# Feed-forwards of a six-layer network: the activations move past loaded weight blocks in five of six column groups

## What is computed

```python
def swiglu(h, w_in, w_out):
    gate, up = jnp.split(h @ w_in, 2, axis=-1)
    return (jax.nn.silu(gate) * up) @ w_out

x = x + 0.5 * rms_norm(swiglu(rms_norm(x, g[0]), ff1_w_in[i], ff1_w_out[i]), g[1])
...
x = x + rms_norm(m, g[3])
x = x + 0.5 * rms_norm(swiglu(rms_norm(x, g[4]), ff2_w_in[i], ff2_w_out[i]), g[5])
```

## Time and profile before

| | |
|---|---|
| median of 3 runs | 2987.64 us (2981.74 to 2991.76) |
| the profiled execution | 2977.27 us |
| its span, first to last instruction | 2975.5 us |
| PE busy | 2938.2 us (99%), 15397 matmuls |
| PE weight loads busy | 2487.7 us (84%) |
| DVE busy | 1804.8 us (61%) |
| ACT busy | 1464.1 us (49%) |
| DMA | 532.97 MB, mean 179 GB/s |

### The profile page before, as it was taken

One profiled execution on the slowest core, in us unless ns is written; L12 is line 12 of the kernel. 1 busy time (PEld: TensorE's weight loads), 2 busy tenths in 40 slices (PEclk: granted clock), 3 DMA queues, 4 the chain that ended last, 5 costly groups with the idle time before them and its releaser, 6 DMA issues.

```text
span 2975.5 us, 38371 instructions
## 1 busy us (share of the span) xinstructions
PE 2938.2 (99%) x15397; PEld 2487.7 (84%) x15397; DVE 1804.8 (61%) x2600; ACT 1464.1 (49%) x2133; POOL 69.3 (2%) x143
## 2 busy tenths in 40 slices
PE   8999999999999999999999999999999999999999
PEld 7889888888888888888888988897888889788887
DVE  6556655556655546765554665469775546977554
ACT  5445544435544444554543464354655434575542
POOL 0000000000000000000000000010000001000000
PEclk9999999999999999999999999999999999999999
DMA  7564555555555555265555635576244557625453
GB/s 247 185 215 134 177 184 193 190 190 199 186 189 181 194 186 191 97 204 185 191 186 182 225 128 186 184 206 214 100 156 156 185 182 208 214 86 184 154 185 129
DMA packets 302403, 532.97 MB, mean 179 GB/s; under 512 B 31074, under 2 KB 125204, under 8 KB 302228
## 3 DMA queue, kind: packets, MB, share of 16 engines
q1 hardware_dynamic: 288964, 511.63, 52.4%
q10 hardware_dynamic: 13264, 18.90, 1.8%
HBM read 528.33 MB, written 1.11 MB: 178 GB/s over the span
## 4 chain that ended last, share of the span: by engine, by line
PE 95%; DVE 2%; DMA 1%; ACT 1%; issue 1%; POOL 0%; ACTq 0%; SPq 0%; POOLq 0%; DVEq 0%
PE bank L744 90%; PE bank L1051 2%; PE bank L1091 1%; PE bank L829 1%; DMA sb_ring<-in_w_xq_dram 1%; DVE sb_parts L1867 0%; PE bank L804 0%; PE bank L812 0%; ACT sb_sc L1510 0%; DMA sb_ring<-in_w_in_dram 0%; ACT sb_parts L1365 0%; DMA sb_ring<-in_ff_w_in_dram 0%; DMA sb_arena<-in_norm_ffn_dram 0%; ACT sb_xn L1477 0%; DVE sb_oT_low L1990 0%
## 5 line engine op out<-in xcount | busy, mean ns | idle before, releaser
L1867 DVE TENSOR_TENSOR sb_parts<-sb_ring,sb_parts 128x2048 fp32r<-128x2048 f32 (+1 forms) x478 | 1092.2, 2289 | 781.6 <-ACT sb_parts L1365 779.6
L744 PE MATMUL bank<-sb_parts,sb_hT_high 128*128 128x512 f32 (+1 forms) x4480 | 1368.2, 391 | 0.7 <-ACT sb_hT_high L1339 0.6
L1365 ACT ACTIVATE sb_parts<-sb_ring 128x2048 fp32r<-128x2048 f32 (+1 forms) x478 | 911.0, 1913 | 812.9 <-PE bank L744 719.0
L744 PEld LDWEIGHTS bank<-sb_parts,sb_hT_high 128*128 128x128 f32 x4480 | 834.9, 188 | 178.8 <-issue 9.1
L744 PE MATMUL bank<-sb_parts,sb_hT_low 128*128 128x512 f32 (+1 forms) x2240 | 852.4, 390 | 0.0
L744 PE MATMUL bank<-sb_parts,sb_hidden_high 128*128 128x512 f32 x1760 | 543.5, 390 | 0.0
L744 PEld LDWEIGHTS bank<-sb_parts,sb_hT_low 128*128 128x128 f32 x2240 | 419.7, 188 | 87.5 <-DVE sb_hT_low L1990 0.5
L744 PEld LDWEIGHTS bank<-sb_parts,sb_hidden_high 128*128 128x128 f32 x1760 | 329.0, 188 | 68.0 <-issue 0.6
L744 PE MATMUL bank<-sb_parts,sb_hidden_low 128*128 128x512 f32 x880 | 342.6, 389 | 0.0
L744 PE MATMUL bank<-sb_hT_high,sb_parts 128*128 128x256 f32 x1408 | 254.9, 283 | 0.0
L744 PEld LDWEIGHTS bank<-sb_hT_high,sb_parts 128*128 128x128 f32 x1408 | 220.1, 192 | 0.0
(11 more groups left out here) (220 smaller groups left out, 1957.8 us busy)
## 6 DMA issues: line engine op xcount, KB each, us to landing
sb_ring<-in_ff_w_in_dram SPq DMA_DIRECT2D x160, 1024.0 KB, 5.1
sb_ring<-in_ff_w_out_dram SPq DMA_DIRECT2D x88, 1024.0 KB, 4.9
sb_ring<-in_w_gate_up_dram SPq DMA_DIRECT2D x40, 1024.0 KB, 5.1
sb_ring<-in_w_in_dram SPq DMA_DIRECT2D x38, 1024.0 KB, 5.1
sb_ring<-in_a_w_qkv_dram SPq DMA_DIRECT2D x24, 1024.0 KB, 5.2
sb_ring<-in_w_down_dram SPq DMA_DIRECT2D x22, 1024.0 KB, 4.9
sb_ring<-in_ff_w_in_dram SPq DMA_DIRECT2D x32, 512.0 KB, 4.9
sb_ring<-in_c_w_qkv_dram SPq DMA_DIRECT2D x12, 1024.0 KB, 5.0
```

Source lines behind the costliest of these rows:

```text
L744: return nc.tensor.matmul(o, lhsT, rhs, start=start, stop=stop)
L1365: nc.scalar.activation(halves(n, slice(0, filled(n))).high, ring[:, raw_in[n], 0:filled(n)], ACT.Copy) \
L1867: V.tensor_tensor(both.low, ring[:, raw_in[n], 0:filled(n)], both.high.bitcast(F32), ALU.subtract) \
```

## The change

In groups 1 to 5 blocks of weights are loaded and hT moves. hT.high and hT.low of a block of 128 now lie side by side in one tensor hT_both, so that one loaded block of high weights meets both in a single matmul of 512 columns: columns 0 to 255 of the bank get high x high, columns 256 to 511 get high x low. The third product, low weights with hT.high, is a matmul of 256 columns into the first half. The results lie in columns (128 hidden columns by 256 rows of x). A group's gate takes four banks j, one per block of 128 hidden columns, and so does its up. ACT copies the second half of a bank to SBUF (`low_half`), DVE adds the first (`gate_sum`, `up_sum`). The transposes of groups 1 to 5 are gone. Row factors in columns come from `turned_factors` (two transposes) and a copy to halves_f; they are multiplied in on the gate. The ups, group 0's included, go without them, and the factor is applied to the output y in `turn` instead. The gate takes its banks from a new list, (5, 6, 7, 4), all four before its first matmul; the up takes all of G.

```diff
-        hT = Split(sb("hT_high", [P, KD, S], F32R), sb("hT_low", [P, KD, S], F32R))
+        hT_both = sb("hT_both", [P, KD, 2, S], F32R)
+        hT = Split(hT_both[:, :, 0, :], hT_both[:, :, 1, :])
...
+        GATE, GATE_AFTER_MEMORY = (Banks(psum, which, owner, taken, readers) for which in ((5, 6, 7, 4), (4, 5, 7, 6)))
...
             def ffn(st):
                 first_rows(st, [(st, "first", h) for h in range(2)], lambda t: (st, "up", 0, t))
+                turned_factors(st, (st, "norm"), 2)
+                for t in range(NT):
+                    for b in range(KD // 2):
+                        pe.wait_ge(dve_read.sem, dve_read.at(((st, "norm"), t, b)))
                 for g in range(1, GROUPS_F):
                     for kind in ("gate", "up"):
-                        banks = [G.take(pe, (st, kind, g, t)) for t in range(NT)]
+                        banks = [((GATE_AFTER_MEMORY if st[0] == "ff3" else GATE) if kind == "gate" else G).take(pe, (st, kind, g, j)) for j in range(4)]
                         for h in range(2):
                             ckey = (st, kind, g, h)
                             arrived(ckey)
                             s = view(ckey)
-                            for t in range(NT):
+                            for j in range(4):
+                                cols = slice(j * P, (j + 1) * P)
                                 for k in range(4):
-                                    ins = split_mm(banks[t][:, :], hT[:, 4 * h + k, t * P:(t + 1) * P], s[:, k, :],
-                                                   h == 0 and k == 0, h == 1 and k == 3)
+                                    kt = 4 * h + k
+                                    if kt:
+                                        mm(banks[j][:, 0:S], s.low[:, k, cols], hT.high[:, kt, :], False, False)
+                                    ins = mm(banks[j][:, :], s.high[:, k, cols], hT_both[:, kt, :, :], kt == 0, kt == KD - 1)
+                                    if kt == 0:
+                                        ins = mm(banks[j][:, 0:S], s.low[:, k, cols], hT.high[:, kt, :], False, False)
...
-                            if kind == "gate" and h == 0:
-                                turned_hidden(st, g - 1, YB)
+                            if g == 1 and kind == "gate" and h == 0:
+                                turned_hidden(st, 0, G)
...
-            def squares(src, c, key):
+            def squares(src, c, key, factor=1.0):
...
+                def low_half(kind, g, j):
+                    act.wait_ge(matmul_done.sem, matmul_done.at((st, kind, g, j)))
+                    last_read = (kind, g, j - 2) if j > 1 else ("gate", g, j + 2) if kind == "up" else ("up", g - 1, j + 2)
+                    if last_read[1]:
+                        act.wait_ge(dve_read.sem, dve_read.at((st, *last_read)))
+                    copy(halves_f[:, j % 2, :], G.of((st, kind, g, j))[:, S:2 * S]).then_inc(act_read.sem, act_read.next((st, kind, g, j)))
...
-                    V.scalar_tensor_tensor(hid_f[:, t, 0:S], G.of((st, "up", 0, t))[:, S:2 * S], row_factor_of(st, t),
-                                           silu[:, t, 0:S], ALU.mult, ALU.mult) \
+                    V.tensor_tensor(hid_f[:, t, 0:S], G.of((st, "up", 0, t))[:, S:2 * S], silu[:, t, 0:S], ALU.mult) \
                         .then_inc(dve_read.sem, dve_read.next((st, "up", 0, t)))
+                factors_in(st, halves_f[:, 6, :])
+
+                def gate_sum(g, j):
+                    dve.wait_ge(act_read.sem, act_read.at((st, "gate", g, j)))
+                    if (g, j) > (1, 1):
+                        dve.wait_ge(act_step.sem, act_step.at((st, "silu", *((g, j - 2) if j > 1 else (g - 1, j + 2)))))
+                    one = halves_f[:, 2 + j % 2, :]
+                    settle(dve, V.tensor_tensor(one, G.of((st, "gate", g, j))[:, 0:S], halves_f[:, j % 2, :], ALU.add),
+                           dve_read, (st, "gate", g, j))
+                    V.tensor_tensor(one, one, halves_f[:, 6, :], ALU.mult).then_inc(dve_step.sem, dve_step.next((st, "summed gate", g, j)))
+
+                def up_sum(g, j):
+                    dve.wait_ge(act_read.sem, act_read.at((st, "up", g, j)))
+                    one = halves_f[:, 4 + j % 2, :]
+                    settle(dve, V.tensor_tensor(one, G.of((st, "up", g, j))[:, 0:S], halves_f[:, j % 2, :], ALU.add),
+                           dve_read, (st, "up", g, j))
+                    dve.wait_ge(act_step.sem, act_step.at((st, "silu", g, j)))
+                    V.tensor_tensor(one, one, silu_columns[:, j, :], ALU.mult).then_inc(dve_step.sem, dve_step.next((st, "hidden", g, j)))
+
+                def low_of(g, j):
+                    dve.wait_ge(act_step.sem, act_step.at((st, "hid high", g, j)))
...
+                def hidden_columns(g):
+                    up_sum(g, 0)
+                    up_sum(g, 1)
+                    low_of(g, 0)
+                    up_sum(g, 2)
+                    low_of(g, 1)
+                    up_sum(g, 3)
+                    low_of(g, 2)
+                    low_of(g, 3)
```

More of the change, by code:

```diff
@@ L1371, in squares_free @@
                     act.wait_ge(squared.sem, squared.count)
-            def squares(src, c, key):
+            def squares(src, c, key, factor=1.0):
                 squares_free()
-                nc.scalar.activation(junk, src, ACT.Square, accum_out=ssum[:, c:c + 1]).then_inc(squared.sem, squared.next(key))
+                nc.scalar.activation(junk, src, ACT.Square, scale=factor, accum_out=ssum[:, c:c + 1]).then_inc(squared.sem, squared.next(key))
             def norm_high(st, t):
@@ new lines, in silu_of @@
+                def silu_of(g, j):
+                    act.wait_ge(dve_step.sem, dve_step.at((st, "summed gate", g, j)))
+                    if g == 1:
+                        act.wait_ge(dve_read.sem, dve_read.at((st, "up", 0, 1)))
+                    else:
+                        act.wait_ge(dve_step.sem, dve_step.at((st, "hidden", g - 1, j)))
+                    nc.scalar.activation(silu_columns[:, j, :], halves_f[:, 2 + j % 2, :], ACT.Silu) \
+                        .then_inc(act_step.sem, act_step.next((st, "silu", g, j)))
@@ L1443, in ffn @@
                 for g in range(1, GROUPS_F):
                     ahead((st, "gate", g, 0))
-                    hidden_high(st, g - 1)
+                    if g == 1:
+                        hidden_high(st, 0)
+                    else:
+                        hidden_columns(g - 1)
                     ahead((st, "gate", g, 1))
-                    for t in range(NT):
-                        act.wait_ge(matmul_done.sem, matmul_done.at((st, "gate", g, t)))
-                        act.wait_ge(dve_read.sem, dve_read.at((st, "up", g - 1, t)))
-                        nc.scalar.activation(silu[:, t, :], G.of((st, "gate", g, t))[:, :], ACT.Silu, scale=row_factor_of(st, t)) \
-                            .then_inc(act_read.sem, act_read.next((st, "gate", g, t)))
@@ L1453, in ffn @@
-                    for h in range(2):
-                        ahead((st, "up", g, h))
+                    ahead((st, "up", g, 0))
+                    low_half("gate", g, 0)
+                    low_half("gate", g, 1)
+                    silu_of(g, 0)
+                    low_half("gate", g, 2)
+                    silu_of(g, 1)
+                    low_half("gate", g, 3)
+                    silu_of(g, 2)
+                    silu_of(g, 3)
+                    ahead((st, "up", g, 1))
                 for m in range(KF // 2 - 1):
@@ L1914, in times_gain @@
                             bank, key = output(st, t, h)
-                            V.tensor_tensor(xn[:, t, half], bank[:, :], gain_row[n % 2][:, half], ALU.mult) \
-                                .then_inc(dve_read.sem, dve_read.next(key))
+                            if st[0] == "mix":
+                                ins = V.tensor_tensor(xn[:, t, half], bank[:, :], gain_row[n % 2][:, half], ALU.mult)
+                            else:
+                                ins = V.scalar_tensor_tensor(xn[:, t, half], bank[:, :], row_factor_of(st, t), gain_row[n % 2][:, half],
+                                                             ALU.mult, ALU.mult)
+                            ins.then_inc(dve_read.sem, dve_read.next(key))
                         def first_half():
@@ L1938, in turn @@
                             dve.wait_ge(matmul_done.sem, matmul_done.at(key))
-                            settle(dve, V.tensor_tensor(x[:, t, half], x[:, t, half], bank[:, :], ALU.add), dve_read, key)
+                            if st[0] == "ff3":
+                                ins = V.scalar_tensor_tensor(x[:, t, half], bank[:, :], row_factor_of(st, t), x[:, t, half], ALU.mult, ALU.add)
+                            else:
+                                ins = V.tensor_tensor(x[:, t, half], x[:, t, half], bank[:, :], ALU.add)
+                            settle(dve, ins, dve_read, key)
```

(17 more changed lines are left out.)

40 lines of the change are left out of this document (28 added, 12 removed).

## The result

The change makes the kernel slower: 3016.43 us (median of 4 runs, 3003.2 to 3026.57) against 2984.69 us of the kernel before in the same rounds (4 runs, 2977.65 to 2991.76). The ratio is 1.0103, 95% interval [1.0074, 1.0133], +32 us. The forecast was 2986.1 us, no change, with a range of 2957 to 3012 us; the time lies above the range.

What follows compares the result with a forecast made beforehand. PE's own time was taken to bound the kernel. Matmuls +21, transposes -46, the bank wait +25 and a covered wait -1.5 made -1.5 us on 2987.64: 2986.1 us, eight-in-ten range 2957 to 3012 us.

Steps and rivals of the forecast that it cites:

- Ten times: +25 us.: Before group 1's gate PE waits for DVE's read of group 0's bank, once in each of ten feed-forwards: +25 us.
- 2.49 us: Length of PE's single wait for DVE's bank read before group 1's gate, 334.12 less 331.63.
- rival (a): The bank wait before group 1's gate costs nothing, because DVE's read comes earlier than today: 2961 us, chance 0.11.
- 320 x (0.2267 + 0.120) = 110.9 us: Matmuls of groups 1 to 5, per feed-forward: 320 pairs of 512 and 256 columns, against 108.8 us before: +2.1 us each.
- rival (d): Weight loads disturb the 256-column matmul slots of groups 1 to 5, ten ns each: 3018 us, chance 0.10.
- the 0.39 and 0.42 us that were allowed: Time per added 256-column operation, per group 16 on ACT (0.39 us) and 20 on DVE (0.42 us); cost nothing.
- (b): Alternating matmul lengths in groups 1 to 5 pack closer, 0.113 us a 256-column slot: 2964 us, chance 0.11.
- (c): DVE frees the up banks late, 1.2 us at 0.85 us an operation, 40 times, +48 us: 3034 us, chance 0.08.
- Rival (e): The 1,600 additional weight loads stay uncovered by matmuls: 3293 us, chance 0.02.
- the page's rule: Skill page: weight loads overlap matmuls in flight only in a different row group; 1,600 additional loads would cost 171 us.

Runs made afterwards that it cites:

- Experiment 2: Kernel before, plus one wait of PE for DVE's read of group 0's first up bank ahead of group 1's gate: 3018.04 us, ratio 1.0128.
- Experiment 1: Changed kernel with each bank taken right before its own first matmul, not all four ahead: 2969.44 us, ratio 0.9965 to the kernel before.
- experiment 7: Kernel before, with PE waiting ahead of group 1's gate only for ACT's earlier read of the same bank: 2989.14 us, ratio 1.0018.
- experiment 6: Changed kernel with banks taken one by one and, per chunk, sixteen long and sixteen short matmuls in runs: 2959.53 us, ratio 0.9928 to the kernel before.
- experiment 4: Changed kernel with banks taken one by one and matmuls of one length in runs of four: 2976.99 us, ratio 0.9973 to the kernel before.
- experiment 3: Changed kernel with matmuls of one length in runs of four, all four banks still taken ahead: 3007.1 us, ratio 1.0079 to the kernel before.

## Why the prediction was wrong, step by step

The forecast was -1.5 us and the medians say +32, so 33.5 us are missing. Two terms miss by about 16 us each, and the wait for L2074 adds 2. Either of the 16 alone would have left the time inside the range (2986 + 16 = 3002 us); both together carried it out.

**The step that failed: "Ten times: +25 us."** The working of this wait held in every part: its place, the bank, DVE last behind two splits, the reads at 0.42 us, and 23.3 us of idle time beside the "2.49 us" each. What failed is that the idle time was taken for the whole cost. Not counted was the clock, some 16 us at the medians, of which the traces put 7 directly behind the waits. None of the sum's terms, and no rival, had the granted clock in it. The trace of before has no idle stretch of PE of such a length within a feed-forward, and its clock is full in every slice; so its rows were silent on what a wait of 2.5 us does to the clock. The prediction bounded the pairs from both sides and the cost of this wait only from below (rival (a)). Experiment 2 shows that the wait does it: alone, in a kernel without pairs, it costs its 26 us and 10 us of clock directly behind it, and the kernel is as slow as the changed one. Experiment 1 takes it away and the stretches behind it are gone, and experiment 7 shows that waits of half the length bring none at these places. The Trainium skill (TensorE: Matmul & The Clock Gate, section HAM oscillation — how this bites in real kernels) tells of this mechanism, waits behind which TensorE starts at the lower clock. By its rule only longer gaps than those of this kernel would do so; the windows above disagree on that, since gaps of 2.3 to 2.7 us did it in some cases.

**The other step that failed, a term mis-sized: "320 x (0.2267 + 0.120) = 110.9 us".** This term, +21 us over ten feed-forwards, measured 351.7 ns a pair, that is +37 us, as much of the miss as the clock and the better shown of the two: experiment 6 gives 14 of the 16 us back. The prediction took the sum of two spacings that each came from a uniform run, and named the absence of a row for alternation. The excess of 5 ns lies inside its upper bound (ten ns, rival (d)), but the mechanism of that rival, loads in the way of 256 slots, is not supported: experiment 6 has exactly as many loads and short matmuls, in runs of sixteen, and goes at 347.3 ns, and in the changed kernel the 256 slots are not stretched at all (116.7 ns for 120). It is the change from short to long that costs, in the first five long matmuls behind it, which is why runs of four cost as much as alternation.

**Right.** The transposes fell to 4 a feed-forward. ACT's and DVE's added operations run at 369 to 425 ns, near the 0.39 and 0.42 us that were allowed, and PE doesn't wait for them at the later gates and ups, with one exception: before the up of group 3 of the first feed-forward it waits 2.2 us for L2074, the reads of group 2's up, since DVE did some 4 us of work of the kernel's start just ahead of them (78.3 to 82.3 us). Rivals (a), (b) and (c) are out: the wait was there, pairs were not closer, and DVE's last read was in time 39 times in 40. Rival (e), and the page's rule beside it, would have shown 171 us or more; pairs of 0.352 us leave no room for it.

**Put together at the medians.** Of +32 us, -9 are matmuls and transposes, +25 are waits, and the rest, about 16, is the clock. Part of that last term isn't settled. Four low stretches behind the waits cost 1.7 us each, 7 us. The remainder comes from low stretches in attention, far from any wait of L2058. By their mean clock about half of the executions of the kernel before have such stretches too, though no trace of one was taken. The changed kernel's profiled execution had two of 23.9 us, and those of experiments 1, 4 and 7 one each, without the wait for DVE. Whether the waits make them more frequent was not shown; all four executions of experiment 2 were at 3016 us or above, which fits it and doesn't prove it.

## What to carry to other kernels

A wait on the engine that bounds the kernel has two prices, its length and what the granted clock does after it, so before costing one by idle time alone look for a wait of that length in any trace and read the clock in the window behind it. Take buffers one by one, right before the first instruction that needs each, when a helper would otherwise ask for all of them at once. And where matmuls of two lengths share weights, put each length into a long run: the sum of the two spacings held in runs of sixteen, not in runs of one or four, because the first five long matmuls behind short ones come late.

## What the chip showed beyond expectation

Idle gaps of 2.3 to 2.7 us in PE brought the granted clock to half for 3.4 us behind three (this change), six (experiment 2) and four (experiment 3) of ten equal waits, and gaps of up to 1.4 us at the same place behind none (experiment 7). Such a stretch costs 1.7 us, two thirds as much again as the wait. The length of a gap doesn't decide it alone: in attention a stretch of 3.4 us begins about 2 us after a gap of 1.2 us in some executions and not in others. There PE also went through 23.9 us at half clock with no idle time in the window (busy 23.90 of 23.90 us). The two levels of time of the kernel before, 11 us apart, and their mean clocks fit such a stretch in half of its executions; that is inferred, since the one that was profiled has none. Matmuls of 512 and 256 columns take 227 and 120 ns in runs of one length and 352 a pair when they alternate; the first five long ones behind a short one are slow, up to 236 ns on average.
